# A two-block layer stack on one core: first memory quarter in two pieces, values stored later, gate columns turned by TensorE, norms' groups 0 and 1 turned together, scans in two

## What is computed

```python
mod = silu(c) @ w_ada + b_ada                      # 6 vectors of 2048: shift1, scale1, gate1, shift2, ...
h = rms_norm(x, g1) * (1 + scale1) + shift1
lru_x, lru_gate, q, k, v, g_a, g_b = split(h @ w_in)
xc = causal_conv4(lru_x)
r, i = sigmoid(block_diag(wa) xc), sigmoid(block_diag(wx) xc)
hs[t] = a[t] * hs[t-1] + u[t]                      # recurrence over tokens, the scan
y_a = (hs * gelu(lru_gate)) @ w_lru_out
y_b = windowed_sink_attention(q, k, v) @ w_attn_out
x = x + gate1 * ((sigmoid(g_a) * y_a + sigmoid(g_b) * y_b) @ w_out)
x = x + gate2 * (relu(norm_and_modulate(x) @ w_ff1) ** 2 @ w_ff2)
x = rms_norm(x, final_g)
for l in range(2):                                 # second block: three attentions on one projection
    k_mem, v_mem = split(mem @ w_mem_kv[l])
    y = concat(fox, dsa, memory attention of x @ w_in_2[l])
    x = layer_norm(ALPHA * x + y @ w_out_2[l])
```

## Time and profile before

| | us |
|---|---|
| median of 3 runs | 2671.2 (2670.3 to 2673.0) |
| the profiled execution | 2674.1 |
| its span, first to last instruction | 2672.3 |

### The profile page before, as it was taken

The page is one execution under the profiler, slowest core; times in us unless marked ns, Lnnn a source line. Parts: engine busy times, 40 slices in busy tenths (PEclk is TensorE's granted clock), DMA queues, the critical chain, the costliest instruction groups (busy, mean ns, idle before and its releaser), DMA issues. The chain is left out here.

```text
span 2672.3 us, 35550 instructions
## 1 busy us (share of the span) xinstructions
PE 2637.4 (99%) x13774; PEld 2232.0 (84%) x13774; DVE 1844.1 (69%) x2519; ACT 1376.8 (52%) x2027; POOL 77.3 (3%) x132
## 2 busy tenths in 40 slices
PE   8999999999999999999999999999999999999998
PEld 7888877777888888888888888888888888888886
DVE  6876888886888676655665566676565656765665
ACT  4137766654544554455445545544554555445543
POOL 0000000000000000000000000100010001000000
PEclk9999999999999999999999999999999999999999
DMA  9985677788988586555565565565546646655463
GB/s 390 409 320 170 191 263 273 263 286 269 363 313 327 181 272 227 191 189 189 189 197 190 183 207 169 176 208 174 166 142 197 228 152 195 211 179 166 144 225 127
DMA packets 164631, 595.33 MB, mean 223 GB/s; under 512 B 19408, under 2 KB 20688, under 8 KB 163952
## 3 DMA queue, kind: packets, MB, share of 16 engines
q1 hardware_dynamic: 158400, 574.00, 63.6%
q0 software_dynamic: 5776, 18.74, 2.2%
q10 hardware_dynamic: 288, 0.33, 0.0%
HBM read 584.53 MB, written 3.21 MB: 220 GB/s over the span
## 5 line engine op out<-in xcount | busy, mean ns | idle before, releaser
L1623 DVE TENSOR_TENSOR both_w<-raw,both_w 128x1024 fp32r<-128x1024 f32 x848 | 1023.3, 1217 | 539.0 <-ACT both_w L1192 534.4
L1192 ACT ACTIVATE both_w<-raw 128x1024 fp32r<-128x1024 f32 x848 | 881.3, 1049 | 610.2 <-PE bank L836 339.5
L873 PE MATMUL bank<-H,both_w 128*128 128x512 f32 x3232 | 778.8, 392 | 0.6 <-ACT both_w L1192 0.5
L873 PEld LDWEIGHTS bank<-H,both_w 128*128 128x128 f32 x3232 | 593.8, 189 | 118.8 <-issue 3.8
L885 PE MATMUL bank<-H,both_w 128*128 128x256 f32 x3232 | 442.9, 286 | 7.5 <-DVE H L2027 4.4
L885 PEld LDWEIGHTS bank<-H,both_w 128*128 128x128 f32 x3232 | 421.8, 191 | 29.3 <-issue 5.7
L831 PE MATMUL bank<-both_w,H 128*128 128x512 f32 x1152 | 291.1, 395 | 10.8 <-ACT both_w L1192 10.8
L831 PEld LDWEIGHTS bank<-both_w,H 128*128 128x128 f32 x1152 | 214.6, 189 | 59.7 <-ACT both_w L1192 9.6
L831 PE MATMUL bank<-both_w,F 128*128 128x512 f32 x1024 | 252.8, 389 | 0.0
L1675 DVE SCALAR_TENSOR_TENSOR raw<-raw,CR 128x1024 f32<-128x1024 f32 x192 | 232.0, 1218 | 15.6 <-DMA raw<-in_ada 15.1
L831 PEld LDWEIGHTS bank<-both_w,F 128*128 128x128 f32 x1024 | 192.2, 188 | 39.9
(11 more groups left out here) (321 smaller groups left out, 2374.3 us busy)
## 6 DMA issues: line engine op xcount, KB each, us to landing
raw<-in_w_in SPq DMA_DIRECT2D x296, 512.0 KB, 3.6
raw<-in_w_ff SPq DMA_DIRECT2D x256, 512.0 KB, 4.2
raw<-in_ada SPq DMA_DIRECT2D x192, 512.0 KB, 5.5
raw<-in_w_out SPq DMA_DIRECT2D x96, 512.0 KB, 4.7
raw<-in_w_sig SPq DMA_DIRECT2D x64, 512.0 KB, 4.8
raw<-in_w_vw SPq DMA_DIRECT2D x48, 512.0 KB, 4.3
raw<-in_w_x SPq DMA_DIRECT2D x32, 512.0 KB, 14.7
raw<-in_w_lru_out SPq DMA_DIRECT2D x32, 512.0 KB, 4.8
```

Of the source, the lines that this page charges most:

```text
L873: ins = pe.matmul(out[i].rearrange("p (a s) -> p a s", a=2), whi[:, s, at_:at_ + 128], both[:, :, kt, :], start=(c == 0 and k == 0), stop= ...
L1192: act.activation(whi[:, s, 0:el.n], raw[el.slot][:, 0:el.n], ACT.Copy).then_inc(s_hi, 1)
L1623: dve.tensor_tensor(wlo[:, s, 0:n], raw[el.slot][:, 0:n], v32(whi[:, s, 0:n]), ALU.subtract).then_inc(s_lo, 1)
```

## The change

It has five parts. (1) The first memory quarter is two elements of 256 KB, each ahead of a weight chunk, and `vec` and `cst` are loaded by GpSimd once four elements are split. (2) `STAGE` becomes two buffers, stored at `lru_weights`, ahead of the recurrence's weights, two of which wait for both stores. (3) The strewn modulation blocks start at chunk 96, and each group of scans gives way once in its middle. (4) The gates' columns are transposed by TensorE, copied by VectorE, and stored as rows; the second mark moves behind `ff1(1)`. (5) In the norms TensorE turns group 1 right after group 0, and ScalarE and VectorE normalise three or four groups before the first spread; the high half becomes a function of its own.

```diff
-    mark("gate", 1)
     for f in range(1, 8):
         ff1(f)
+        if f == 1:
+            mark("gate", 1)
         ff2(f - 1)
...
-        if n < 8 and n % 2 == 0:
-            stream.append(Elem("mem", CH, ("mem", 2, n // 2), g=2, kt=n // 2))
+        if n < 2:
+            stream.append(Elem("mem", CH // 2, ("mem", 2, 2 * n), g=2, kt=2 * n))
+        elif n < 8 and n % 2 == 0:
+            stream.append(Elem("mem", CH, ("mem", 2, 2 * n), g=2, kt=2 * n))
...
-                due += 0 if n < 88 or 268 <= n < 290 else 0.5 if n < 152 else 0.72
+                due += 0 if n < 96 or 268 <= n < 290 else 0.5 if n < 152 else 0.72
...
-    PG = at("PG", [128, 2, 512], o_bt)
+    PG, GT = at("PG", [128, 2, 512], o_bt), at("GT", [16, 128], o_bt)
...
-    STAGE = at("STAGE", [128, 2, 512], o_tg + 4096)
+    STAGE = [at("STAGE0", [128, 2, 512], o_pt), at("STAGE1", [128, 2, 512], o_tg + 4096)]
...  (TensorE, turned)
             for g in range(4):
-                yield
+                if g != 1:
+                    yield
...  (TensorE, the marks)
+                elif st[1] == "gate":
+                    n = st[2]
+                    clear("T")
+                    pe.wait_ge(s_mod, 24 if n else 18)
+                    c = 80 if n else 32
+                    pe.transpose(pT[0:NB, 0:128], mod[:, c:c + NB], ident).then_inc(s_gt, 1)
+                    held["T"] = (s_gsb, n + 2)
...  (ScalarE, norm)
-            normalised(n, 0)
-            normalised(n, 1)
+            for g in range(3):
+                normalised(n, g)
             spread_out(n, 0)
+            high_halves(n, 0)
+            spread_out(n, 1)
             feed(order[begin + 4])
-            normalised(n, 2)
+            high_halves(n, 1)
             normalised(n, 3)
-            for g in range(1, 4):
-                spread_out(n, g)
-                feed(order[begin + 4 + g])
+            feed(order[begin + 5])
+            spread_out(n, 2)
+            high_halves(n, 2)
+            feed(order[begin + 6])
+            spread_out(n, 3)
+            high_halves(n, 3)
+            feed(order[begin + 7])
...  (ScalarE, evac)
             elif kind == "pre":
-                if j:
-                    act.wait_ge(s_vst, 16 * j)
-                act.activation(STAGE[:, :, :], ...)
+                if j == 0:
+                    act.wait_ge(s_cr, 1)
+                act.activation(STAGE[j][:, :, :], ...)
...
-        act.dma_start(cst[:, 0:C_DUP], d_cst[:, 0:C_DUP]).then_inc(s_cst, 16)
-        act.dma_start(vec[:, :], d_vec).then_inc(s_vec, 16)
...  (VectorE, scan)
             for b in range(4 * q, 4 * q + 4):
+                if b == 4 * q + 2:
+                    yield
                 dve.tensor_tensor_scan(...)
...  (VectorE, norm)
-            normalised(n, 0)
-            normalised(n, 1)
+            for g in range(4):
+                normalised(n, g)
             spread_out(n, 0)
-            normalised(n, 2)
-            normalised(n, 3)
+            spread_out(n, 1)
             low_halves(n, 0)
-            spread_out(n, 1)
             feed(order[begin + 4])
             low_halves(n, 1)
+            spread_out(n, 2)
             feed(order[begin + 5])
-            spread_out(n, 2)
             low_halves(n, 2)
+            spread_out(n, 3)
             feed(order[begin + 6])
-            spread_out(n, 3)
+            low_halves(n, 3)
             feed(order[begin + 7])
-            low_halves(n, 3)
...  (VectorE, the marks)
+                elif st[1] == "gate":
+                    n = st[2]
+                    dve.wait_ge(s_gt, n + 2)
+                    if n:
+                        dve.wait_ge(s_z0, 4)
+                        dve.wait_ge(s_z1, 4)
+                    dve.tensor_copy(GT[:, :], pT[0:NB, 0:128]).then_inc(s_gsb, 1)
...  (GpSimd, gate_rows)
+            pool.wait_ge(s_gsb, n + 2)
...
-            pool.dma_start(gates_d[n].rearrange("b p -> p b"), mod[:, c:c + NB],
-                           allow_slow_non_contiguous=True).then_inc(s_gs, 16)
+            pool.dma_start(gates_d[n], GT[:, :]).then_inc(s_gs, 16)
...  (GpSimd, start)
+        pool.wait_ge(s_hi, 4)
+        pool.dma_start(vec[:, :], d_vec).then_inc(s_vec, 16)
+        pool.dma_start(cst[:, 0:C_DUP], d_cst[:, 0:C_DUP]).then_inc(s_cst, 16)
...  (GpSimd, lru_weights)
-                    for c in range(4):
+                    pool.wait_ge(s_ev["pre"], 2)
+                    for l in range(2):
+                        pool.dma_start(values_d[l], STAGE[l][:, :, :]).then_inc(s_vst, 16)
+                    for c in (0, 3, 1, 2):
+                        if c == 1:
+                            pool.wait_ge(s_vst, 32)
                         pool.dma_start(LW[c][:, :], d_lru[c]).then_inc(s_lw, 16)
...
-            if un.kind == "pre":
-                pool.wait_ge(s_ev["pre"], un.j + 1)
-                pool.dma_start(values_d[un.j], STAGE[:, :, :]).then_inc(s_vst, 16)
```

More of the change, by code:

```diff
@@ L270, in _plan @@
         elif s[0] in ("mem", "rep"):
-            stream.append(Elem(s[0], CH, s, g=s[1], kt=s[2]))
+            stream.append(Elem(s[0], CH, s, g=s[1], kt=4 * s[2] if s[0] == "mem" else s[2]))
         elif s[0] == "unit" and not s[1].part and s[1].kind != "pre":
@@ L661, in _build @@
         tensors[f"M{i}"] = (MH[i], ML[i], M1[:, :, :, :] if i else M0[:, 0:3:2, :, :])
-        ready[f"M{i}"] = lambda kt, i=i: (s_lo, mem_no[i, kt // 4])
+        ready[f"M{i}"] = lambda kt, i=i: (s_lo, mem_no[i, 4 * (kt // 4)])
         tensors["MS"] = (Hhi, Hlo, H[:, :, :, :])
-        ready["MS"] = lambda kt: (s_lo, mem_no[2, kt // 4])
+        ready["MS"] = lambda kt: (s_lo, mem_no[2, 2 * (kt // 2) if kt < 4 else 4 * (kt // 4)])
         tensors[f"Y{i}"] = (Yh, Yl, YY[:, 0:4:3, :, :])
@@ L694, in source @@
         if el.kind == "mem":
-            return d_mem[:, 4 * el.kt:4 * el.kt + 4, :].rearrange("p b s -> p (b s)")
+            return d_mem[:, el.kt:el.kt + el.n // S, :].rearrange("p b s -> p (b s)")
         src, u, c = el.src
@@ L1023, in first_norm @@
             held["T"] = (s_rvb, 1)
-            yield from ticks(2)
+            yield
             for g in range(4):
@@ L1193, in feed @@
                 elif el.kind == "mem":
-                    q = el.kt
+                    blocks = slice(el.kt, el.kt + el.n // S)
                     act.wait_ge(s_raw[el.slot], el.landed)
@@ L1199, in feed @@
                         act.wait_ge(s_pv, 48)
-                    act.activation(MH[el.g][:, 4 * q:4 * q + 4, :], raw[el.slot][:, :].rearrange("p (b s) -> p b s", b=4),
+                    act.activation(MH[el.g][:, blocks, :], raw[el.slot][:, 0:el.n].rearrange("p (b s) -> p b s", s=S),
                                    ACT.Copy).then_inc(s_hi, 1)
@@ L1408, in spread_out, with high_halves @@
             ins.then_inc(s_ea, 1)
+        def high_halves(n, g):
             act.wait_ge(s_ea, 4 * n + g + 1)
@@ L1516, in evac @@
             elif kind == "pre":
-                if j:
-                    act.wait_ge(s_vst, 16 * j)
-                act.activation(STAGE[:, :, :], bank[:, un.bank:un.bank + 2, :], ACT.Copy).then_inc(s_ev["pre"], 1)
+                if j == 0:
+                    act.wait_ge(s_cr, 1)
+                act.activation(STAGE[j][:, :, :], bank[:, un.bank:un.bank + 2, :], ACT.Copy).then_inc(s_ev["pre"], 1)
             elif kind in by_token:
@@ L1624, in low @@
             else:
-                q = el.kt
-                dve.tensor_tensor(ML[el.g][:, 4 * q:4 * q + 4, :], raw[el.slot][:, :].rearrange("p (b s) -> p b s", b=4),
-                                  v32(MH[el.g][:, 4 * q:4 * q + 4, :]), ALU.subtract).then_inc(s_lo, 1)
+                blocks = slice(el.kt, el.kt + el.n // S)
+                dve.tensor_tensor(ML[el.g][:, blocks, :], raw[el.slot][:, 0:el.n].rearrange("p (b s) -> p b s", s=S),
+                                  v32(MH[el.g][:, blocks, :]), ALU.subtract).then_inc(s_lo, 1)
         def token_rows(el):
@@ L2321, in gate_rows @@
         def gate_rows(n):
+            pool.wait_ge(s_gsb, n + 2)
             if n == 0:
                 pool.wait_ge(s_pv, 32)
-                pool.wait_ge(s_mod, 18)
             else:
                 pool.wait_ge(s_ev["res"], 4)
-                pool.wait_ge(s_mod, 24)
-            c = 80 if n else 32
-            pool.dma_start(gates_d[n].rearrange("b p -> p b"), mod[:, c:c + NB],
-                           allow_slow_non_contiguous=True).then_inc(s_gs, 16)
+            pool.dma_start(gates_d[n], GT[:, :]).then_inc(s_gs, 16)
             pool.wait_ge(s_gs, 16 * (n + 1))
             pool.dma_start(GR[:, :], bass.AP(tensor=gates_d.tensor, offset=n * D, ap=[[0, 128], [1, D]])).then_inc(s_gr, 16)
+        pool.wait_ge(s_hi, 4)
+        pool.dma_start(vec[:, :], d_vec).then_inc(s_vec, 16)
+        pool.dma_start(cst[:, 0:C_DUP], d_cst[:, 0:C_DUP]).then_inc(s_cst, 16)
         pool.dma_start(hot[:, :], d_hot).then_inc(s_hot, 16)
@@ L2379, in gpsimd @@
                 continue
-            if un.kind == "pre":
```

(4 more changed lines are left out.)

## The result

The changed kernel takes 2657.5 us (2657.4 to 2657.9, four runs) beside 2671.3 us for the kernel before (2670.3 to 2673.0, four runs): ratio 0.9948, interval 0.9936 to 0.9961. The forecast was 2656.4 us, range 2652.0 to 2664.4. The profiled execution took 2657.4 us, its span 2655.4 us.

The account below looks back on a forecast made before the run. TensorE, busy 99% of the span, bounds the kernel, except that transfers set the time up to about 161 us. Gains of 2.5 + 2.4 + 1.9 - 0.6 + 8.6 = 14.8 us give 2656.4 us, range 2652 to 2664.4.

Parts of the forecast that it names:

- Start: First stage: first matmul about 1.9 us earlier, worth 0 on the path; bounds 0.8 us gained to 0.8 lost.
- Values stored later: Transfer-bound first stage: two 512 KB stores leave it, 2.5 us gained, bounds 1.7 and 2.6.
- Rival C: Saturated first stage ends no earlier, as VectorE's sums or TensorE's projection take over: 2.5 us lost, 2658.9 us; chance 0.07.
- Blocks and scans: First attention: low half 2.4 us sooner; 1.8 and 0.9 us gained, 0.3 lost, net 2.4; bounds 0 and 3.0.
- the third, 0.97 us: First attention, TensorE's wait up to 328.50 us behind a modulation block: forecast gone, 0.9 us gained.
- Gate columns: At the gates: TensorE's 1.89 us wait at 670.74 us goes, 1.9 us gained; TensorE's transposes lose 0.6.
- no wait of ScalarE above 4 us near 645 us: Sign for the gates: no ScalarE wait for a weight chunk above 4 us near 645 us.
- Second gate's rows: Rows land at T + 15 us, T the end of the ff1 unit; price 0, at worst 1.3 us.
- Norms: Three norms: no TensorE wait at a low half; 2.5 + 1.9 + 1.4 + 2.8 = 8.6 us gained, bounds 4 and 10.
- The clock's 2.8 us: First two norms: granted clock back at 1.00 with the waits gone, 1.4 us each; bounds 0 and 1.7 each.
- Rival A: Norms' wait replaced: TensorE waits for a split or the clock falls; half of 8.6 us lost, 2660.7 us; chance 0.18.
- The sum: Whole kernel: 2.5 + 2.4 + 1.9 - 0.6 + 8.6 = 14.8 us off the 2671.2 us median, 2656.4 us.

Follow-up runs that it names:

- the start alone: Kernel before with the first memory quarter in two pieces, constants on GpSimd's queue and first norm's groups turned one chunk earlier: 2672.3 us, ratio 1.0001.
- the kernel before, again: The kernel before, unchanged, profiled a second time: 2671.8 us.
- the norms alone: Kernel before with only the norms' new order on three engines: 2662.2 us, ratio 0.9964.
- six traces with the slow store: Kernel before, profiled twice, and with stores, start, blocks or norms alone; stage before `G` 286.13, 284.90, 283.99, 283.96, 283.96, 284.40 us.
- the gate's part alone: Kernel before with only the gate columns' part of the change: 2670.6 us, ratio 0.9996.

## Why the prediction came out right, step by step

- **Start, 0 forecast.** It costs 0.23 us alone and 0.35 us beside the other parts in the first stage, within the bound of 0.8, and gives 0.28 us in the ninth, which the prediction did not have and whose cause is open. The working reads the 1.2 GHz level off weight loads of 0.38 us; the granted clock of the windows view is 1.00 from 8 to 14 us, so that the two don't agree there. No term rests on it. The step that held: in front of a stage that the transfers fill, an earlier start of TensorE gives nothing.
- **Values stored later, 2.5 us.** Measured 2.34, or 2.06 with what the start costs there. 1 MB at the row's 409 GB/s was the right measure. Rival C is out.
- **Blocks and scans, 2.4 us.** Measured 2.5, but mis-sized inside: the sum took the block and the two scans as equal parts, and the blocks give 2.2, the scans 0.26. The order of the waits was right except that the third, 0.97 us, keeps 0.56: a wait at 324 us, where the prediction wanted none. With the scans whole it is gone and one of 0.65 us stands at 312 us, so cutting them mostly moves a wait.
- **Gate columns, 1.9 us gained and 0.6 lost.** This term failed twice. The wait of 1.89 us stands in one profiled execution; in six traces it is worth 0.6 us in the mean. And the turns cost 0.15 us, not 0.6: I took 0.3 us for one, while the eight of the earlier trace rows take 1.04 us together, 0.13 each. The net was forecast at 1.3 us and is 0.45. The part has a use that I did not see: it carries the blocks, which alone lose 1.75 us at the second gate. And the sign "no wait of ScalarE above 4 us near 645 us" could not fail, since the store is no longer there; beside the store at 800.57 us ScalarE's longest wait for a weight chunk is 2.7 us, to 810.62 us.
- **Second gate's rows.** Forecast T + 15.0, measured T + 14.9 us; VectorE waits 3.95 us, TensorE not. By the fit of the Trainium skill (DMA: Bandwidth & Descriptors, Anatomy of one DMA) I estimate 2.0 us for the store and 4.4 us for the read, T + 11.1 us; the trace has 1.6 us for the store and 8.2 us for the read (3.3 and 5.3 us at the first gate), and the measurement decides.
- **Norms, 8.6 us.** Measured 9.85 us by medians, in which stands what chance adds to the kernel before. By stages, without falls of the clock: 3.9 + 2.1 + 2.4 = 8.4 us, where the waits alone had been put at 2.5 + 1.9 + 1.4 = 5.8. The mechanism held: the last low half was forecast 14.8 us behind the first transpose (913.3 less 898.5 us) and ends 14.4 us behind it. The waits themselves were priced too low. The first norm gives 1.4 us more because smaller waits followed the large one (0.19 and 0.23 us in the timeline of the start alone, at 928.22 and 939.84 us), and the third 1.0 more, in part because a wait of 0.46 us for a high half at 2160.53 us went with the low half's. The idle time in the view is less than what a wait costs: with the matmuls of the kernel before, again, and of the norms alone set side by side, the large wait of the first norm costs 2.7 us for 2.46 in the view, the two small ones some 0.45 us each for 0.19 and 0.23, and three steps behind them, which are in no view, 0.4 us together. The clock's 2.8 us was the wrong size: two of six traces with the old order in the kernel before have a fall at the second norm, 1.56 us each, and in the first it costs 0.1 to 0.4, for there TensorE's slower pace takes the place of those smaller waits. Rival A is out, as its two tell-tales are absent.
- **The sum.** Stage by stage, the kernel before without a fall of the clock and without the wait at 670 us stands 13.1 us above the changed one: 2.1 + 2.5 + 3.9 + 2.1 + 2.4 + 0.3 - 0.15, where the 0.3 is the ninth stage, which goes with the start. Its lowest run, 2670.3 us, is 12.9 us above 2657.4 us, as if it had neither; it has no trace. With what its executions add by chance the median of all 61 runs is 15.0 us above, that of the first four 13.8. The forecast of 14.8 us lay between, and that it came so near is in part luck: terms too large (the gate's by 0.85 us, the clock's) and too small (the waits of the norms, 5.8 us for 8.4) made up for each other.

## What to carry to other kernels

When two engines each walk a list in order, look at the order of their lists first when a wait stands at the end of a stretch: here the order is worth 8.9 us, and the earlier transposes 1.6 with it and nothing without it. A wait that stands in one profiled execution has to be seen in a second before it is priced, above all where a transfer releases it or the granted clock falls behind it. Of two edits that look independent, ask whether one makes late what the other makes quick: the blocks without the quick store give back 1.75 of the 2.2 us that they gain. And the idle time that a view shows before an instruction can be less than what the wait costs.

## What the runs showed of the hardware

- The granted clock fell to its 1.2 GHz level for some 3 to 4 us behind waits of TensorE of only 1.8 to 4.8 us, and behind the same waits in another execution of the same kernel it did not fall. A fall cost 1.5 us where TensorE worked on without waits behind it, 0.5 us in the first attention, and 0.1 to 0.4 us in the first norm, where VectorE was late as well.
- A store of 8 KB in 2048 elements of 4 bytes took 12 to 15 us from issue to the end of GpSimd's wait, and the loads of other queues slowed beside it: from 648 to 656 us all transfers of the core ran at 30 GB/s, with its DMA engines busy 0.52 of the time, and from 988 to 996 us, beside the second such store, at 70 GB/s and 0.91. At the first gate ScalarE waited 6.4 to 8.3 us before it could copy the next weight chunk, in each of the six traces with the slow store; beside the second, it waited no longer than 1.7 us before any. The same 8 KB in rows of 512 bytes took 3.6 and 1.9 us by the same measure, and the transfers ran at 250 GB/s from 800 to 808 us and at 224 from 995 to 1003 us. With the gate's part alone, whose store has left that place too, it is 264 GB/s from 648 to 656 us.

```profile
648.00:656.00 8.00, 8.00 (x37) 6.60 (x37) 4.65 (x6) 2.15 (x3) 0.00 (x0) 1.00 0.52 30
```

- The two stores of 512 KB landed in 7.1 us within the full stage and in 3.7 and 4.9 us behind it.
